# A fused three-block transformer kernel: gate tiles and projections in banks of their own, another order of GLA and SWA, shorter head norms

## What is computed

```python
x = x + short_conv_mixer(rms(x, attn_norm[0]), ...)
x = x + conv_ffn(rms(x, ffn_norm[0]), ...)
k, v, c = split(rms(x, kv_norm) @ w_kvf)         # keys (rms per head), values, log-gate sums
q, g = split(rms(x, attn_norm[1]) @ w_qg)        # 16 heads of 64, q rms per head
x = x + (forgetting_attention(q, k, v, c) * sigmoid(g)) @ w_out
x = x + conv_ffn(rms(x, ffn_norm[1]), ...)
h = rms(x, norm_mix_g) ; proj = h @ w_in         # all projections of the last block
# GLA: 4 heads, dk 128, dv 256, chunks of 64, one pass forward and one backward
z = lr @ up + bias ; log_g = max(log_sigmoid(z) / 16, -0.5)
o = gla(q, k, v, log_g_f) + flip(gla(flip(q), flip(k), flip(v), flip(log_g_b)))
y_gla = (rms(o, out_g) * silu(r)) @ w_o_gla
# SWA: 8 query heads of 128, 2 key/value heads, window 128, rope, rms per head, a sink per head
y_swa = softmax_with_sink(rope(rms(q)) @ rope(rms(k)).T / sqrt(128), window) @ v @ w_o_swa
x = x + (sigmoid(gate_a) * y_gla + sigmoid(gate_b) * y_swa) @ w_out
x = x + (silu(ffn_gate) * ffn_up) @ w_ffn_out
```

## Time and profile before

| | us |
|---|---|
| median of three runs | 2284.39 |
| the three runs | 2275.85, 2284.39, 2285.44 |
| the profiled execution | 2275.83 |
| its span, first to last instruction | 2273.9 |
| PE busy | 2155.7 (95%) |
| DVE busy | 1209.4 (53%) |
| ACT busy | 432.6 (19%) |
| POOL busy | 1277.8 (56%) |
| mean granted TensorE clock | 0.983 |

### The profile page before, as it was taken

One profiled execution on the slowest core, in us unless ns is written; L12 is line 12 of the kernel. 1 busy time (PEld: TensorE's weight loads), 2 busy tenths in 40 slices (PEclk: granted clock), 3 DMA queues, 4 the chain that ended last, 5 costly groups with the idle time before them and its releaser, 6 DMA issues.

```text
span 2273.9 us, 29246 instructions
## 1 busy us (share of the span) xinstructions
PE 2155.7 (95%) x10847; PEld 1794.3 (79%) x10847; DVE 1209.4 (53%) x1610; ACT 432.6 (19%) x874; POOL 1277.8 (56%) x907
## 2 busy tenths in 40 slices
PE   6999999999789999999999979998789999999999
PEld 4888888888688877888888768877767888888887
DVE  5567877712456667777741365445574346334301
ACT  2002111100323343211110152212122012111000
POOL 3776767666443335676756634434233766767664
PEclk9999999999999999999999989999989999999999
DMA  3333333233322222333323312213111333333232
GB/s 119 101 102 103 101 93 101 79 89 110 84 75 66 75 84 73 94 93 100 94 77 93 111 51 63 66 47 84 37 56 47 102 95 95 98 95 99 70 101 78
DMA packets 366708, 193.21 MB, mean 85 GB/s; under 512 B 6416, under 2 KB 363120, under 8 KB 366624
## 3 DMA queue, kind: packets, MB, share of 16 engines
q1 hardware_dynamic: 363168, 186.67, 28.3%
q10 hardware_dynamic: 3456, 5.40, 0.8%
HBM read 189.91 MB, written 2.13 MB: 84 GB/s over the span
## 4 chain that ended last, share of the span: by engine, by line
PE 80%; DVE 12%; ACT 3%; issue 3%; POOL 0%; ACTq 0%; DMA 0%; DVEq 0%; POOLq 0%
PE PS L476 19%; PE PS L477 19%; PE PS L478 19%; DVE W L1528 2%; PE PS L739 2%; PE PS L741 2%; PE PS L740 2%; PE PS L723 2%; PE PS L724 2%; PE PS L725 2%; PE PS L624 1%; DVE PROB L1595 1%; PE PS L626 1%; PE PS L625 1%; DVE BC L1747 1%
## 5 line engine op out<-in xcount | busy, mean ns | idle before, releaser
L461 POOL TENSOR_TENSOR RING<-RAW,RING 128x1024 fp32r<-128x1024 f32 (+1 forms) x354 | 869.3, 2456 | 29.5
L459 POOL TENSOR_SCALAR RING<-RAW 128x1024 fp32r<-128x1024 f32 (+1 forms) x354 | 373.9, 1056 | 621.5 <-PE PS L741 164.9
L476 PE MATMUL PS<-XH,RING 128*128 128x512 f32 x1352 | 531.4, 393 | 4.8 <-DVE XT L2069 2.6
L477 PE MATMUL PS<-XL,RING 128*128 128x512 f32 x1352 | 528.2, 391 | 0.0
L478 PE MATMUL PS<-XH,RING 128*128 128x512 f32 x1352 | 527.9, 390 | 0.0
L476 PEld LDWEIGHTS PS<-XH,RING 128*128 128x128 f32 x1352 | 254.9, 188 | 61.6 <-DVE XT L2069 3.0
L477 PEld LDWEIGHTS PS<-XL,RING 128*128 128x128 f32 x1352 | 255.0, 189 | 53.2 <-issue 1.2
L478 PEld LDWEIGHTS PS<-XH,RING 128*128 128x128 f32 x1352 | 254.9, 189 | 53.2
L458 POOL TENSOR_TENSOR COL<-COL 128x1 f32<-128x1 f32 x195 | 43.4, 222 | 322.7 <-PE PS L478 322.7
L478 PE MATMUL PS<-HH,RING 128*128 128x512 f32 x528 | 205.7, 390 | 0.0
L477 PE MATMUL PS<-HL,RING 128*128 128x512 f32 x528 | 205.7, 390 | 0.0
(11 more groups left out here) (304 smaller groups left out, 3469.2 us busy)
## 6 DMA issues: line engine op xcount, KB each, us to landing
RAW<-in_ffn_w_up SPq DMA_DIRECT2D x88, 512.0 KB, 3.6
RAW<-in_w_in SPq DMA_DIRECT2D x53, 512.0 KB, 3.6
RAW<-in_w_ffn_in SPq DMA_DIRECT2D x44, 512.0 KB, 3.6
RAW<-in_ffn_w_down SPq DMA_DIRECT2D x32, 512.0 KB, 3.8
RAW<-in_a_w_in SPq DMA_DIRECT2D x24, 512.0 KB, 3.5
RAW<-in_w_kvf SPq DMA_DIRECT2D x17, 512.0 KB, 3.8
RAW<-in_b_w_qg SPq DMA_DIRECT2D x16, 512.0 KB, 3.7
RAW<-in_w_ffn_out SPq DMA_DIRECT2D x16, 512.0 KB, 3.8
```

What stands on the lines that cost most here:

```text
L459: pool.tensor_scalar(WH[s][:, 0:nk, :], RAW[s][:, 0:nk, :], 1.0, 1.0, ALU.mult, ALU.mult).then_inc(high_done, 1)
L461: pool.tensor_tensor(WL[s][:, 0:nk, :], RAW[s][:, 0:nk, :], WH[s][:, 0:nk, :].bitcast(F32), ALU.subtract).then_inc(split_done, 1)
L476: pe.matmul(o, WH[s][:, k, :], xh[:, k0 + k, :], start=first and k == 0, stop=False)
L477: pe.matmul(o, WH[s][:, k, :], xl[:, k0 + k, :], start=False, stop=False)
```

## The change

1. Ring slots: the stages "quads", "late" and "attn_out" begin in slot 2 and "lr" in slot 3, not in slot 0.
2. Attention: in odd pairs `turn` comes one token piece later.
3. Head norms: instead of the squared row scale, the kernel keeps EPS divided by it, so one operation makes the mean plus that epsilon, and the multiplication by the row scale falls away (the scale cancels between bank and norm). `newton` has two operations, not three, everywhere.
4. GLA gates: UP and LRT are held four times, once in each group of 32 partitions (eight DMAs instead of two, four products instead of one), the eight tiles go to banks of their own as far as there are any (`Z_BANK`), ZC has eight buffers and SP six. The first scores wait for two gate tiles instead of eight.
5. GLA order: scores follow dense piece 9 of the same head; the turned output comes before the last piece; ACT takes gates 2 to 5 in one batch with one pair of table loads, and does `gla_high` ahead of `gla_r`; beside the last head three sigmoids come earlier.
6. SWA: doubles 0 to 5 go to banks 0, 4, 6, 0, 0, 0 and the one above each (`X_BANK`); turns stand behind the third and fourth block; three dense pieces stand between scores and turned probabilities; `merge1` has one unit more (gate B's first), taken from `merge2`.

The core of the diff:

```diff
-        ph["quads"] = wphase(4, 1, [...])
+        ph["quads"] = wphase(4, 1, [...], first=2)
-        ph["lr"] = wphase(4, 1, [(w_in, 0, KT, lambda i: G_LR)])
+        ph["lr"] = wphase(4, 1, [(w_in, 0, KT, lambda i: G_LR)], first=3)
...
                         token_piece(quad, 2, 0)
+                        token_piece(quad, 2, 1)
                         turn(p)
-                        token_piece(quad, 2, 1)
                         feature_major(0, p + 1)
...
+        Z_BANK = (2, 3, 6, 7, 4, 5, 6, 7)
+        X_BANK = (0, 4, 6, 0, 0, 0)
...
-                for k in range(first, first + 2):
-                    if k >= 2:
-                        pe.wait_ge(sem("z_read"), k - 1)
-                    t = ZT[k]
-                    pe.matmul(PS[:, 2 + k % 2, :], UP[:, t * P:(t + 1) * P], LRT[:, :], start=True,
+                for k in range(first, last):
+                    if k < 4:
+                        pe.wait_ge(sem("lr"), k + 1)
+                    elif k == 4:
+                        pe.wait_ge(sem("token_scale"), 2)
+                    elif k >= 6:
+                        pe.wait_ge(sem("z_read"), k - 3)
+                    t, r = ZT[k], LOW[k % 4]
+                    pe.matmul(PS[:, Z_BANK[k], :], UP[r, t * P:(t + 1) * P], LRT[r, :], start=True,
...
+                gate_tiles(0, 4)
+                gla_dense(0, 4)
+                gla_dense(0, 5)
+                gate_tiles(4, 8)
+                for n in range(6, 10):
+                    gla_dense(0, n)
...
+                for i in range(GH):
                     gla_scores(i, 0)
                     gla_turn_keys(i, 0)
-                    gla_dense(i + 1, 0)
+                    filler(i, 10)
                     gla_values(i, 0, 0)
...
+                    for n in range(18, 21):
+                        filler(i, n)
                     gla_turn_out(i)
+                    filler(i, 21)
...
             def gla_high(i):
+                act.wait_ge(sem("g_cum"), 2 * GH)
...
+                gla_gates(0, 2)
+                gla_decay(0)
                 gla_v(0, 0)
+                gla_decay(1)
                 gla_v(0, 1)
+                gla_gates(2, 6)
                 gla_r(0, 0)
                 for i in range(GH):
                     gla_keys(2 * i)
+                    gla_r(i, 1)
                     gla_keys(2 * i + 1)
+                    if i == 0:
+                        gla_gates(6, 8)
                     if i < GH - 1:
                         gla_decay(2 * i + 2)
                     gla_square(i)
                     if i < GH - 1:
                         gla_decay(2 * i + 3)
+                        gla_v(i + 1, 0)
+                        gla_v(i + 1, 1)
+                    gla_high(i)
+                    if i < GH - 1:
+                        gla_r(i + 1, 0)
...
-                link(dve.tensor_tensor(v, v, rr, ALU.mult))
-                link(dve.tensor_scalar(v, v, -0.5, 1.5, ALU.mult, ALU.add))
-                ins = dve.tensor_tensor(out_, r, v, ALU.mult)
+                link(dve.scalar_tensor_tensor(v, v, -0.5, rr, ALU.mult, ALU.mult))
+                ins = dve.scalar_tensor_tensor(out_, v, 1.5, r, ALU.add, ALU.mult)
...
-                link(dve.tensor_tensor(SVAR, SVAR, r2, ALU.mult))
-                dve.tensor_scalar(SVAR, SVAR, EPS, None, ALU.add).then_inc(sem("sw_v"), 1)
+                dve.scalar_tensor_tensor(SVAR, SVAR, 1.0 / P, eps, ALU.mult, ALU.add).then_inc(sem("sw_v"), 1)
...
-                link(dve.tensor_tensor(SHR, SHR, rt, ALU.mult))
...
+                swa_scores(0, 0)
+                swa_dense(5, 0)
+                swa_turn(6)
+                swa_dense(5, 1)
+                swa_dense(5, 2)
+                swa_turn_probs(0, 0)
+                swa_turn(7)
+                swa_dense(5, 3)
+
+                swa_scores(0, 1)
+                swa_weigh(0, 0)
+                merge1(0)
+                merge1(1, 0)
+                swa_turn_probs(0, 1)
+                merge1(1, 1)
```

On DVE the order of the first two softmaxes is then:

```diff
+                swa_max(0, 0)
+                swa_scale(0, 0)
+                swa_rotate(6)
+                swa_sums(8)
+                swa_turned(0, 0)
+                swa_norm(8)
+                swa_rotate(7)
+
+                swa_max(0, 1)
+                swa_scale(0, 1)
+                swa_low(0, 0)
+                swa_sums(9)
+                swa_norm(9)
+                swa_turned(0, 1)
+                og_read(0)
```

More of the change, by code:

```diff
@@ L727, in half_unit, with token_block @@
                     mm.then_inc(unit_done, 1)
-            def token_block(p, j, t, half_sem, free):
+            def token_block(p, j, t, half_sem, free, bank=0):
                 s = p.slot(j)
@@ L917, in swa_turn @@
+            def swa_dense(x, t):
+                free = {0: [(sem("ga_read"), 5), (sem("ga_read"), 4)],
+                        1: [(sem("g_st"), 2 * GH * (NCH - 1))] * 2, 2: [(sem("g_on"), GH * TB)] * 2,
+                        3: [(sem("sw_x"), 1), (sem("sw_x"), 2)],
+                        4: [(sem("sv"), 1), (sem("sv"), 2)], 5: [(sem("sw_x"), 7), (sem("sw_x"), 8)]}[x]
+                token_block(ph["swa"], 2 * x, t, sem("sw_half"), free, X_BANK[x])
             def swa_turn(n):
@@ L957, in swa_weigh, with merge1 @@
                 mm.then_inc(sem("sw_pv"), 1)
-            def merge1(j, half=None):
+            def merge1(j, *halves):
                 name, m = M1[j]
@@ L967, in merge1 @@
                     pe.wait_ge(sem("g_ylow"), 2 * GH)
-                for h in (0, 1) if half is None else (half,):
+                for h in halves or (0, 1):
                     half_unit(ph["merge1"], j, h, bank, xh, xl, free)
@@ L996, in swa @@
[L996 to L1003 removed]
+                        if x in (1, 2, 3) and t >= 2:
+                            swa_turn(2 * (x - 1) + t - 2)
+                swa_scores(0, 0)
+                swa_dense(5, 0)
@@ L1838, in gla @@
                 dve.wait_ge(unit_done, ph["lr"].unit(0, 0) + 1)
-                r = slice(0, 2 * GATE_RANK)
-                dve.tensor_tensor(LRT[:, :], PS[r, 4, :], W[0][r, 0:S], ALU.mult).then_inc(sem("lr"), 1)
+                low = LOW[0]
+                for r in LOW:
+                    dve.tensor_tensor(LRT[r, :], PS[low, 4, :], W[0][low, 0:S], ALU.mult).then_inc(sem("lr"), 1)
                 link(dve.memset(RESET[:, :], 1.0))
@@ new lines, in swa @@
+                swa_rotate(8)
+                swa_turned(0, 2)
+                og_read(2)
+                swa_max(0, 3)
+                swa_scale(0, 3)
+                og_read(3)
+                swa_low(0, 2)
+                swa_rotate(9)
+                swa_turned(0, 3)
+                og_read(4)
+                swa_max(1, 0)
+                swa_scale(1, 0)
+                swa_low(0, 3)
+                ga_read(5)
+                swa_turned(1, 0)
+                swa_max(1, 1)
+                swa_scale(1, 1)
@@ new lines, in swa @@
+                ga_read(6)
+                swa_low(1, 0)
+                swa_turned(1, 1)
+                swa_max(1, 2)
+                swa_scale(1, 2)
+                swa_low(1, 1)
+                og_read(5)
+                swa_turned(1, 2)
+                swa_max(1, 3)
+                swa_scale(1, 3)
+                swa_low(1, 2)
+                og_read(6)
+                ga_read(7)
+                swa_turned(1, 3)
+                gb_read(0)
+                swa_low(1, 3)
+                og_read(7)
```

415 lines of the change are left out of this document (184 added, 231 removed).

## The result

The changed kernel takes **2186.7 us** (median of 4, 2186.2 to 2187.8) against 2280.3 for the kernel before (4 runs, 2275.9 to 2285.4): ratio 0.9589, 95% interval 0.9563 to 0.9616. By the two profiled executions the span fell from 2273.9 to 2184.5 us, 89.4 less, where the prediction summed 78.5.

A forecast was written before the change was run, and what follows sets the result against it. The prediction took TensorE, busy 95% of the span, as the bound, with its waits and lowered clock to gain. Terms of 78.5 us off the profiled 2275.8 gave 2197; half of 8.6 added made 2201, range 2182 to 2238.

The forecast's parts named there:

- Attention, first part: Attention up to the first scores: ring-slot wait gone, norm waits slightly shorter, some clock back; 9.8 us gained (6.4 to 12).
- Pairs: Attention's eight pairs: the later turn removes three PROB waits, 9.0 us, plus 4 of clock; 13.0 us gained (9.0 to 17.4).
- GLA: GLA stage: most waits go, some new ones come, clock and gate tiles gain; 27.7 us gained (17 to 34).
- Row groups: GLA gate tiles: eight 32-row tiles in four row groups overlap on TensorE; 3.5 us gained (0 to 6).
- SWA projections: Sliding-window projections: own banks and later turns remove 8.9 us of waits and 6.1 of clock; 15.0 us gained (10 to 18.6).
- Softmaxes: Softmaxes with first merge units: old waits go, a new one of 8 us comes; 13 us gained (8 to 21).
- The added 4 us: Whole kernel: half of the 8.6 us by which the profiled execution lay below its runs' median, added to 2197.
- A: Rival, whole kernel: held VectorE gives half back, 30 to 40 us less gained, 2235 us; chance 0.14.
- B: Rival, whole kernel: the waits go but the clock's losses of 18.8 us stay, 2220 us; chance 0.08.
- C: Rival, GLA gates: first head waits as long as before, no overlap in row groups; 2215 us; chance 0.13.
- D: Rival, whole kernel: no new waits, row groups at their bound; 2182 to 2190 us; chance 0.12.
- E: Rival, softmaxes: TensorE waits at merge banks and SPROB in every one; slower, 2290 to 2360 us; chance 0.03.

The follow-up runs named there:

- experiment 1: Changed kernel with only the ring slots put back (quads, late, attn_out and lr begin in slot 0 again): 2196.6 us.
- experiment 4: Kernel before with only the short head norms of the change (attention and sliding window): 2247.8 us, ratio 0.9836 to the kernel before.
- experiment 3: Changed kernel with only the long head norms of before put back (seven small operations instead of four): 2210.3 us.
- 7: Changed kernel with one small operation more in each head norm, ahead of ScalarE's root: 2197.0 us.
- 8: Changed kernel with two small operations more in each head norm, behind ScalarE's root: 2204.1 us.
- experiment 2: Changed kernel with only the turn of the second head's probabilities put back ahead of the next token piece: 2187.0 us.
- experiment 11: Changed kernel with ScalarE's first batch of GLA gates cut from four to two, the other four in the second batch: 2181.4 us.
- experiment 6: Changed kernel with the projection doubles 1 and 2 in banks 0 and 1 again, turns still one block later, norms short: 2200.6 us.

## Why the prediction was right, and where it was not

**Right in the total, 14 us high.** 11 us of it are terms of the sum, 4 the step from the profiled execution to the median. The time lies in the stated range, but not in the 2192 to 2212 that had the chance of 0.50: four of the five terms were too small, and only the softmaxes' was too large.

**Attention, first part** (9.8, was 13.6). The slots: right, 8.0 by experiment 1. The row scale's wait, put 0.4 shorter, is 1.3 longer, since POOL's split now runs into that norm. The step that failed is the norms', "their end is set by POOL's second split, 0.6 us each". That is so for the norm of before, whose timeline I had read, and not for the short one: 6.0 us instead of 1.2 (experiment 4; experiments 3, 7 and 8 show why).

**Pairs** (13.0, was 16.4). Right by size, wrong by cause. "The change puts one more token piece ahead of these transposes ... so 3 x 3.0 = 9.0 goes" and "VectorE's work does not move": it did move. In VectorE's order a head norm stands ahead of the second head's maxima. In the second pair the last scaled probability comes 19.7 us behind the first score in experiment 3 (675.40 to 695.05) and 16.6 in experiment 2 (668.09 to 684.68): 3.1 us of the 3.8 us wait there; the other two pairs with such a wait are not shown. The turn alone gives 8.8, the norms alone 16.4, both 16.4. That the sum came near is luck: two edits could each pay for the same wait, and I had counted the one that turned out to add nothing.

**GLA** (27.7, was 30.3). The wait for turned keys: 3.4 predicted, 3.9 measured, and experiment 11 shows it to be the four-gate batch. The gate sums behind the first head: 2.5 taken, 1.0 measured. Row groups: 3.5 taken, 5.5 measured (7.7 to 2.15); I had nearly halved the bound of 6 on the strength of a two-group row. These three differences (-0.5, +1.5, +2.0) make up the 2.6 us by which GLA did better, within 0.4. The waits for YGL went, as said. What the order and the buffers gave apart from these was not tried piece by piece.

**SWA projections** (15.0, was 19.1). "Turns 2 and 4 each wait 1.8": they wait 0.4 each: the short norm again, which alone gives 12.0 of the 19.1 (experiment 4). Banks: needed, as said (experiment 6).

**Softmaxes** (13, was 11.0). The one new wait was named with its place and semaphore, at 8 (6 to 10) us; it is 10.2. POOL had five tiles to split, not four. Its clock cost was put at 2.1: the next half unit ran at a clock of 0.50 and took 5.26 us, where others there take 2.8 to 3.2. So the clock stood at 0.95 in this stretch, not at the 0.99 that the prediction named as a sign.

**The added 4 us** had no ground. Runs of the new kernel do not scatter as those of the old one (1.6 us against 9.6); the last section has what is known of why.

**Rivals.** A and B did not happen: no more held waits than named, and the clock came back, 0.994. C did not: the row groups overlap. D's time is right, its mechanism half: row groups near their bound, but three waits of 3.9, 10.2 and 1.3 us were new. E did not happen: seven of the eight windows have no wait.

**VectorE and POOL.** The prediction had every VectorE instruction that touches SBUF alone wait for POOL. That is too wide: reciprocals and sums were not held (the last paragraph below).

## What to carry to other kernels

A chain of small VectorE operations beside POOL's splits has no length of its own: lay both timelines over each other and see between which POOL instructions each operation falls. One operation fewer can be worth nothing or a whole split, and where it is in the norm of every chunk, it changes the waits of three stages. Before you credit a reordering with a wait, ask what else in the change shortens the same chain; two edits that both cover one wait add up to one. Where an operation must run beside a long run of POOL, give it to ScalarE or put ahead of it whatever TensorE wants first.

## What the runs showed of the hardware

**The same wait may or may not cost the clock.** TensorE waited 3.0 us for YGL three times in the kernel before and three times in the kernel with short norms alone. The 12 matmuls of a half unit behind each, in the kernel before and then in the other (the counts take in what runs on at the edges):

```profile
1403.97:1406.90 2.93, 2.93 (x17) 2.18 (x15) 2.93 (x2) 0.59 (x1) 2.85 (x2) 1.00 0.62 179
1455.66:1458.60 2.94, 2.94 (x15) 2.15 (x13) 2.94 (x2) 0.59 (x1) 2.86 (x2) 1.00 0.66 177
1507.49:1511.90 4.41, 4.41 (x14) 3.25 (x12) 4.31 (x4) 0.59 (x1) 2.80 (x2) 0.64 0.52 133
```

```profile
1383.59:1388.10 4.51, 4.51 (x16) 3.34 (x14) 3.59 (x3) 0.59 (x1) 1.75 (x1) 0.64 0.60 173
1438.07:1442.60 4.53, 4.53 (x16) 3.38 (x14) 3.59 (x3) 0.59 (x1) 1.75 (x1) 0.62 0.63 166
1492.58:1497.20 4.62, 4.62 (x16) 3.42 (x14) 3.59 (x3) 0.59 (x1) 1.75 (x1) 0.62 0.63 172
```

The clock was down behind one of three in the first and behind all three in the second, with the same work of TensorE ahead of them. From the scores behind the wait to the end of the half unit the three take 14.4 us in the first kernel and 21.1 in the other. That is most of the 7.6 us that GLA took more in experiment 4, and it fits the spread of the kernel before: its 21 executions beside the experiments lie between 2275.9 and 2286.0 us, those near 2276 at a mean clock of 0.983 and those from 2284 up at 0.975 or 0.978. The changed kernel has none of these three waits, and its four runs lie within 1.6 us. The profiled execution of before was a lucky one: it is 4.5 us below the median of its four runs and some 9 below the medians of those beside the experiments. A gain read from it is too small by as much, which is the 9.2 us between the two readings of experiment 4. What decides it was not tried. The Trainium skill, "TensorE: Matmul & The Clock Gate", Part 1, says that the number of slow matmuls at a kernel's start varies from run to run; these rows show the like in the middle of one.

**Which VectorE operations POOL holds.** On SBUF alone TENSOR_TENSOR and SCALAR_TENSOR_TENSOR (2.25 us each at 128x8) and TENSOR_SCALAR (2.23) were held until a POOL instruction ended, where 0.17 is usual; a RECIPROCAL of 128x4 (0.18 us at 1574.77) and a TENSOR_REDUCE (0.67 us at 1582.47) ran through beside POOL's splits, and so did what reads PSUM (0.68 us at 1581.87).
